# Triangular inverse of the chunked recurrence: blocks of 32 instead of 64 on TensorE, and an order that counts changes of tile size

## The reference, cut to what matters

```python
def step(S, inp):
    r_t, w_t, k_t, v_t, kk_t, b_t = inp
    sa = jnp.einsum('bhvk,bhk->bhv', S, kk_t)
    S = (S * w_t[:, :, None, :] - sa[..., None] * b_t[:, :, None, :]
         + v_t[..., None] * k_t[:, :, None, :])
    return S, jnp.einsum('bhvk,bhk->bhv', S, r_t)
```

## Time and profile before

| | |
|---|---|
| time, median of 3 runs | 3736.47 us (3733.08 to 3736.66) |
| the profiled execution | 3741.04 us, span 3739.3 us |
| mean granted TensorE clock | 0.97 |
| PE busy in the span | 3506.3 us (94%) |
| DVE busy | 1892.1 us (51%) |
| ACT busy | 945.0 us (25%) |
| DMA | 177.54 MB, mean 47 GB/s |

### The profile page before, as it was taken

The page is one execution under the profiler, slowest core; times in us unless marked ns, Lnnn a source line. Parts: engine busy times, 40 slices in busy tenths (PEclk is TensorE's granted clock), DMA queues, the critical chain, the costliest instruction groups (busy, mean ns, idle before and its releaser), DMA issues.

```text
span 3739.3 us, 63595 instructions
## 1 busy us (share of the span) xinstructions
PE 3506.3 (94%) x28813; PEld 2205.1 (59%) x28813; DVE 1892.1 (51%) x2750; ACT 945.0 (25%) x1867; POOL 49.4 (1%) x114
## 2 busy tenths in 40 slices
PE   7998879989999999789999999998899698999988
PEld 2445655549989899444444444445566345777753
DVE  2037746435555554645555540115999653444524
ACT  3006640125455555220000000100111302233310
POOL 2000000000000000100000000000000000000000
PEclk9999999989999999899999999999999899999999
DMA  6001003200000000321111121113111012010021
GB/s 229 0 14 54 1 23 135 81 6 18 4 18 4 4 4 4 110 94 64 67 57 45 43 93 40 57 51 96 34 34 56 11 63 58 23 34 23 1 84 62
DMA packets 110626, 177.54 MB, mean 47 GB/s; under 512 B 5379, under 2 KB 66562, under 8 KB 109714
## 3 DMA queue, kind: packets, MB, share of 16 engines
q1 hardware_dynamic: 101218, 141.59, 11.3%
q10 hardware_dynamic: 9136, 31.87, 2.4%
HBM read 147.23 MB, written 26.21 MB: 46 GB/s over the span
## 4 chain that ended last, share of the span: by engine, by line
PE 85%; DVE 9%; ACT 4%; DMA 2%; issue 1%; ACTq 0%; SPq 0%; DVEq 0%
PE psum_all L66 83%; ACT sbuf_all L75 3%; DVE sbuf_all L94 3%; DVE sbuf_all L84 2%; DVE sbuf_all L102 2%; PE psum_all L69 1%; ACT L75 1%; DMA sbuf_all<-in_w_mod 1%; DVE sbuf_all L91 0%; DMA sbuf_all<-in_gla_w_out 0%; DVE sbuf_all L108 0%; DMA sbuf_all<-in_w_up 0%; DVE sbuf_all L97 0%; DMA yd_spill<-sbuf_all 0%; DMA sbuf_all<-in_conv_w_in 0%
## 5 line engine op out<-in xcount | busy, mean ns | idle before, releaser
L66 PE MATMUL psum_all<-sbuf_all 64*64 64x64 f32 (+12 forms) x28042 | 3406.6, 306 | 183.4 <-ACT sbuf_all L75 57.6
L66 PEld LDWEIGHTS psum_all<-sbuf_all 64*64 64x64 f32 (+5 forms) x28042 | 2120.3, 153 | 1446.2 <-issue 1032.3
L75 ACT ACTIVATE sbuf_all<-psum_all 128x512 f32<-128x512 f32 (+5 forms) x925 | 409.4, 462 | 1543.4 <-PE psum_all L66 1428.9
L94 DVE SCALAR_TENSOR_TENSOR sbuf_all<-sbuf_all 128x1040 f32<-128x1040 f32 (+8 forms) x571 | 623.5, 1094 | 25.1 <-PE psum_all L66 4.9
L84 DVE TENSOR_TENSOR sbuf_all<-sbuf_all 128x512 f32<-128x512 f32 (+10 forms) x593 | 470.3, 817 | 165.1 <-ACT sbuf_all L75 121.3
L75 ACT ACTIVATE sbuf_all<-sbuf_all 128x64 f32<-128x64 f32 (+10 forms) x454 | 260.9, 584 | 856.4 <-DVE sbuf_all L78 355.2
L78 DVE COPY sbuf_all<-psum_all 128x256 f32<-128x256 f32 (+5 forms) x137 | 71.0, 526 | 472.7 <-PE psum_all L66 459.3
L75 ACT ACTIVATE sbuf_all<-psum_all,sbuf_all 128x1280 f32<-128x1280 f32 (+5 forms) x212 | 163.9, 781 | 342.4 <-PE psum_all L66 326.1
L84 DVE TENSOR_TENSOR sbuf_all<-sbuf_all,psum_all 128x512 f32<-128x512 f32 (+3 forms) x160 | 102.0, 640 | 274.4 <-PE psum_all L66 273.3
L108 DVE COPY_PREDICATED sbuf_all<-sbuf_all,psum_all 128x256 f32<-128x256 int32 (+2 forms) x296 | 145.6, 493 | 159.5 <-PE psum_all L66 154.8
L69 PE MATMUL psum_all<-sbuf_all 128*128 128x128 f32 (+2 forms) x771 | 109.5, 281 | 38.5 <-DVE sbuf_all L84 9.5
(11 more groups left out here) (19 smaller groups left out, 140.6 us busy)
## 6 DMA issues: line engine op xcount, KB each, us to landing
sbuf_all<-in_w_mod SPq DMA_DIRECT2D x12, 2048.0 KB, 8.3
sbuf_all<-in_w_up SPq DMA_DIRECT2D x22, 1024.0 KB, 7.7
sbuf_all<-in_w_in SPq DMA_DIRECT2D x6, 2048.0 KB, 8.9
x_spill<-sbuf_all SPq DMA_DIRECT2D x16, 512.0 KB, 2.9
sbuf_all<-in_conv_w_in SPq DMA_DIRECT2D x16, 512.0 KB, 6.3
sbuf_all<-in_gla_w_in SPq DMA_DIRECT2D x8, 1024.0 KB, 5.3
sbuf_all<-in_w_down SPq DMA_DIRECT2D x4, 1792.0 KB, 7.4
hid_spill<-sbuf_all ACTq DMA_DIRECT2D x9, 512.0 KB, 2.6
```

What stands on the lines that cost most here:

```text
L66: return self.e.matmul(out, lhsT, rhs, start=start, stop=stop, skip_group_check=True)
L75: return self.e.activation(out, in_, func, bias=bias, scale=scale, **kw)
L94: return self.e.scalar_tensor_tensor(out, a, s, b, op0, op1) if self.e is not None else Unissued()
```

## The change

Levels 1 to 4 combine blocks that lie within blocks of 32. Before, they were computed on the whole 64x64 matrices, of which all but the diagonal blocks of 32 are zero. Now D and E of these levels are kept compact: 128 partitions by 4 chunks by 32 columns, four blocks of 32 on the partitions (two heads, two diagonal blocks each), and each matmul is 32x32 weights by 32 columns on one quarter of the partitions (`QUARTERS`). So `first_turn` and `level_y` have 16 small matmuls where there were 8, `level_de` 32 where there were 16.

The last level, from blocks of 32 to blocks of 64, becomes two products of 8 small matmuls, `last_y` and `last_e`, from one quarter of the partitions to its neighbour. `spread` (VectorE, two predicated copies) puts the compact E back on the diagonal of the full one, `last_turn` (VectorE) copies the first product, and `last_out` (VectorE) puts the new corner into the full E. `de_out` of the last level on ScalarE falls away. The copies out of PSUM are half as wide as before at levels 1 to 4. The masks are rebuilt for blocks of 32 on GpSimd in the stage before, in more and smaller operations (16 instead of the 4 that copied `half_level`).

The costs in the scheduler's table are new (for instance 280 ns for `level_y` in place of 500), TensorE is charged `CHANGE` = 90 ns when a step has another tile size than the one before it, and `PACE` is 3600 instead of 5000. So the order of the steps is another one on all three engines.

```diff
-SCAN_LEVELS = range(1, 6)
+SCAN_LEVELS = range(1, 5)
+QUARTERS = [(slice(32 * n, 32 * n + 32), 32 * (n % 2)) for n in range(4)]
...
-PACE = 5000
+PACE = 3600
...
+BY_32 = ("first_turn", "level_y", "level_de", "last_y", "last_e")
+OTHER_TILES = ("key_norms", "key_spread", "gates")
+CHANGE = 90
...
-        step("t", 500, ("first_turn", gi), ("first", gi))
-        step("s", 390, ("first_out", gi), ("first_turn", gi))
+        step("t", 280, ("first_turn", gi), ("first", gi))
+        step("s", 300, ("first_out", gi), ("first_turn", gi))
         for li in SCAN_LEVELS:
...
+            step("t", 280, ("level_y", gi, li), ("first_out", gi) if li == 1 else ("de_out", gi, li - 1))
+            step("v", 330, ("turn", gi, li), ("level_y", gi, li))
+            step("t", 530, ("level_de", gi, li), ("turn", gi, li))
+            step("s", 390, ("de_out", gi, li), ("level_de", gi, li))
+        done = ("de_out", gi, SCAN_LEVELS[-1])
+        step("v", 400, ("spread", gi), done)
+        step("t", 280, ("last_y", gi), done)
+        step("v", 300, ("last_turn", gi), ("last_y", gi))
+        step("t", 280, ("last_e", gi), ("last_turn", gi))
+        step("v", 330, ("last_out", gi), ("last_e", gi), ("spread", gi))
+        step("t", 500, ("solve", gi), ("last_out", gi), ("turned_out", gi, 0), ("turned_out", gi, 1))
...
+                    change = e == "t" and tile_mode(name[0]) != mode
+                    choices.append((max(at, free[e] + CHANGE * change), due[name], name[1:], name))
...
             for u in range(4):
-                for rows in HALVES:
-                    done = te.matmul(bank[rows, u * C:(u + 1) * C], g["A"][rows, u, 0:64], g["D"][rows, u, :])
+                for rows, b in QUARTERS:
+                    done = te.matmul(bank[rows, u * 32:u * 32 + 32], g["A"][rows, u, b:b + 32], g["D"][rows, u, :])
             done.then_inc(*T.tick("level_y", gi, li))
...
+            old = lambda rows, b, u: g["E"][rows, u, b:b + 32] if li == 1 else g["E32"][rows, u, :]
             for u in range(4):
-                for rows in HALVES:
-                    done = te.matmul(bank[rows, 256 + u * C:256 + (u + 1) * C], turn[rows, u, :], g["E"][rows, u, :])
+                for rows, b in QUARTERS:
+                    te.matmul(bank[rows, u * 32:u * 32 + 32], old(rows, b, u), turn[rows, u, :])
+            for u in range(4):
+                for rows, b in QUARTERS:
+                    done = te.matmul(bank[rows, 128 + u * 32:160 + u * 32], turn[rows, u, :], old(rows, b, u))
             done.then_inc(*T.tick("level_de", gi, li))
+        elif kind == "last_y":
...
+            for u in range(4):
+                for (rows, _), (to, b) in zip(*sides(STREAMS[GROUPS[gi][0]][1])):
+                    done = te.matmul(bank[to, u * 32:u * 32 + 32], g["A"][rows, u, b:b + 32], g["D"][rows, u, :])
+            done.then_inc(*T.tick("last_y", gi))
...
+        elif kind == "spread":
...
+            for b in range(2):
+                ve.predicated(g["E"][:, :, 32 * b:32 * b + 32], K.side_mask[:, b, :].bitcast(I32).unsqueeze(1).broadcast_to([P, 4, 32]),
+                              g["E32"]).then_inc(*V.tick("spread", gi))
```

More of the change, by code:

```diff
@@ L1077, in project_pool @@
             ge.wait_ge(*G.now())
-            ge.copy(K.half_level[d][rows], side[rows, 0:6, h * 64:(h + 1) * 64]).then_inc(*G.tick())
+            ge.copy(K.first_level[d][rows], side[rows, 0, h * 64:(h + 1) * 64]).then_inc(*G.tick())
+    ge.wait_ge(*G.now())
+    ge.memset(K.side_mask, 0.0).then_inc(*G.tick())
+    for n in range(4):
+        rows, cols = slice(32 * n, 32 * n + 32), slice(32 * n, 32 * n + 32)
+        for d in range(2):
+            ge.wait_ge(*G.now())
+            ge.copy(K.turn_mask[d][rows], K.level["lower" if d == 0 else "upper"][rows, 1:5, cols]).then_inc(*G.tick())
+        ge.wait_ge(*G.now())
+        ge.copy(K.quarter_ident[rows, :], K.ident[rows, cols]).then_inc(*G.tick())
+        ge.wait_ge(*G.now())
+        ge.memset(K.side_mask[rows, n % 2, :], 1.0).then_inc(*G.tick())
     ge.wait_ge(*G.now())
@@ L1141, in group_chunks, with tile_mode @@
     return chunk_order(s)[4 * n:4 * n + 4]
-PACE = 5000
+PACE = 3600
 HALF = ((0, 640), (640, 1280))
 EVACUATED = {"key_norms": "key_roots", "key_spread": "key_scale", "gates": "gate_out", "bonus": "bonus_out", "products": "mask", "first_turn": "first_out",
-             "turned": "turned_out", "level_y": "turn", "level_de": "de_out", "solve": "solve_out"}
+             "turned": "turned_out", "level_y": "turn", "level_de": "de_out", "last_y": "last_turn", "last_e": "last_out",
+             "solve": "solve_out"}
+BY_32 = ("first_turn", "level_y", "level_de", "last_y", "last_e")
+OTHER_TILES = ("key_norms", "key_spread", "gates")
+CHANGE = 90
+TURN_READ = {"turn": "level_de", "last_turn": "last_e"}
+def tile_mode(kind):
+    return 32 if kind in BY_32 else 128 if kind in OTHER_TILES else 64
 def scan_steps():
@@ L1545, in scan_vector @@
     chunked = lambda x: x.rearrange("p (n t) -> p n t", t=C)
-    turns, last_turn = K.turn_level, {}
+    turn_user = {}
     c3, lw3, t13, aa3, kk3 = (chunked(x) for x in (cc, lw, t1, aa, K.kk))
@@ L1829, in scan_pool @@
         for turn in side:
-            ge.copy(turn, K.half_ident.unsqueeze(1).broadcast_to([P, 4, C])).then_inc(*K.scan.g.tick("turn_levels"))
+            ge.copy(turn, K.quarter_ident.unsqueeze(1).broadcast_to([P, 4, 32])).then_inc(*K.scan.g.tick("turn_levels"))
 def scan_sync(K, sy):
```

115 lines of the change are left out of this document (73 added, 42 removed).

## The result

The changed kernel takes 3939.89 us (median of 4 runs, 3937.37 to 3943.67) against 3736.56 us for the kernel before on the same chip: ratio 1.0545, 95% interval 1.0527 to 1.0564. It is 5.4% slower, 203 us, where 76 us less was forecast. The profiled execution has a span of 3935.6 us. The end of the recurrence moved from 1509.9 to 1709.3 us, 199 us later, so the whole loss lies in the changed stretch; the forecast had it at 1434.

A forecast was written before the change was run, and what follows sets the result against it. The prediction took TensorE, busy 94% of the span, as the bound: 3741 us, less 101 (127 saved, 26 for changes), plus 25 of waits, gives 3665; 4.6 us lower for the median, 3661, range 3625 to 3712.

The forecast's parts named there:

- the round of four: 32x32 level work on TensorE: four records, one on each quarter, in 32 ns; 153 us with two-quarter rounds, against 280 before.
- a term that the prediction put at nothing: TensorE's granted clock in the recurrence: a fall below 0.98 was named as possible and priced at nothing.
- 26 us of changes: TensorE's order in the recurrence: 288 more changes of tile size at 0.09 us each, bounds 0 and 43 us.
- 25 of waits: New TensorE waits for other engines in the recurrence: 25 us added, bounds 0 and 50.
- The signs named for being wrong: 32x32 windows under 100 or 65 records a us, VectorE or ScalarE over 25% of the chain, or clock clearly below 0.98.
- Rival 2: 32x32 work on TensorE: issuing eight instructions makes a round about 44 ns, not 32; 3704 us, chance 0.10.
- The bound above: Upper limit for a round of four on TensorE: 58 ns, if smaller size gives nothing but four still overlap.
- Rival 3: 32x32 work on TensorE: quarters don't overlap as halves do, a round takes 64 ns; 3774 us, chance 0.05.
- Rival 4: TensorE's small matmuls: every record keeps its 29 ns whatever its size; about 4005 us, chance 0.01.
- Rival 1: VectorE and ScalarE take back TensorE's gain through new waits of 55 to 85 us; middle 3706 us, chance 0.15.
- The last sign of error: TensorE's granted clock clearly below the 0.98 of before, since TensorE would be less busy; priced at nothing.

The follow-up runs named there:

- e11_busy64: The changed kernel with every product on blocks of 32 moving 64 columns in place of 32, same matmul count and order, values wrong; 3938.63 us, ratio 1.054.
- e9_busy: The changed kernel with all its matmuls kept, every product on blocks of 32 moving 128 columns in place of 32, values wrong; 3997.69 us, ratio 1.0695.
- e12_busy64c0: The changed kernel with 64 columns in each product on blocks of 32 and CHANGE = 0, values wrong; 3889.87 us, ratio 1.0402.
- e2_wide: The changed kernel with half the matmuls on blocks of 32, each moving 64 columns, values of half the chunks wrong; 3705.0 us, ratio 0.9908.
- e1_lab: The kernel before with stretches of matmuls that wait for nothing ahead of the recurrence, for its trace only; 640 records of 32x32 took 15.8 us.
- e3_change0: The changed kernel with CHANGE = 0, so 595 changes of tile size instead of 375; 3894.37 us, ratio 1.042.
- e5_wide4: The changed kernel with a quarter of the matmuls on blocks of 32, each moving 128 columns, values of three chunks of four wrong; 3654.09 us, ratio 0.9778.
- e6_realcost: The changed kernel with the scheduler's TensorE costs set to what the instruction supply gives and PACE 5000; 3948.68 us, ratio 1.0567.
- e8_lab2: The kernel before with longer stretches of matmuls that wait for nothing, for its trace; 2560 records on four quarters took 70.5 us.

## Why the prediction was wrong

**The step that failed** is the round of four under "TensorE, term by term": 4160 rounds on four quarters at 32 ns and 640 on two at 32 ns, 153 us. The array does start a round of four in 33 ns. But the level work has 8960 matmuls, 17920 records, 35840 instructions with the loads: 140 blocks, at 3.45 us each 483 us. Put in the place of the 153, that makes 697.9 - 280 + 483 = 901 us for the recurrence, and 897.3 were measured.

That it comes so near is luck. By this sum the 32x32 work takes 483 us and the rest 418; in the trace they take 379 and 517 (table under e11_busy64). So the term of 153 us was 226 too small, not 330: small matmuls also live on blocks that came in while the others ran. The other 100 us are the rest at the lower clock, a term that the prediction put at nothing; in e9_busy, with the clock up, the same work takes 416. That the two trade against each other at nearly the same total e11_busy64 and e12_busy64c0 show, and so the count of instructions is what the loss goes back to. The sum for e2_wide, 70 blocks, is near in the same way (697.9 - 280 + 242 = 660, 663.5 measured), and it leaves out the 26 us of changes and 25 of waits that the prediction added. The row was in the profile all along: 226 packets of the instruction queue, and for 1000 to 1100 us of the kernel before

```profile
q8 instruction: 21, 0.34, 1.5%
```

a packet every 4.8 us; unbroken 64x64 work takes one every 3.74 (256 x 14.6 ns). There was next to nothing to gain by more and shorter matmuls. The signs named for being wrong show it too: at 128 records in 3.45 us there are 37 records of 32x32 a us, far under the 65 of rivals 3 and 4, though for neither's reason, and the idle time before them is 126 us, 115 of it issue, where tens were to be right. I read transfers as data only, and wrote that none is near the path.

**Why the rest doesn't make up for it.** If the supply had run on evenly beside all work, the 213 packets of the recurrence would have needed 213 x 3.45 = 735 us, and not 897. But at full clock the 64x64 work takes an instruction every 14.6 ns, hardly slower than the supply gives them, and only about two blocks are ahead, so there is little reserve for the small matmuls. This is worked out from e1_lab; e3_change0 and e12_busy64c0 agree, where more mixing gave back 45 and 49 us.

**Rival 2** named the issue of eight instructions, but priced it at 44 ns a round, from halfway to the bound of 58 ns. The bound was taken from pairs, four instructions; the same rate for eight is 117 ns, and the measured mean of a long stretch is 110 (70.5 us for 640 rounds). So it named nearly the right thing, at 12 of the 78 ns a round that it cost. The bound above was wrong by treating the round, not the instruction, as the unit. **Rival 3** fell: four quarters do overlap. **Rival 4** gave 4005 us by 29 ns a record, near in size, and for small records in a long row nearly right as a mean (27.5); but its reason, a floor between starts, is not what happens: within a burst records start every 8 ns. The rule of the Trainium skill that I cited there, from "TensorE: Matmul & The Clock Gate", is contradicted across tiles as it was in the earlier trace rows. The Trainium skill does describe the blocks, in "Runtime: NRT & Kernel Launch", section "Instruction fetch mechanics": 256 instructions in 16 KiB, fetched in sequence while others are executed. It calls the cost mostly hidden; here it is 1.2 to 2.6 us a block for such tiles.

**Rival 1**, VectorE and ScalarE, fell: their waits together didn't grow (26 us against 28), and e5_wide4 reached 3654 with the same copies.

**Terms that held.** Changes: in TensorE's records the first start after a change from 64x64 to 32x32 comes 0.098 us later than normal at full clock, the way back 0.095, against my 0.09. Predicated copies of 128x128: 303 ns (305). The copies of `spread`: 315 ns, where I took 250. ScalarE's 128x256: 386 (384). The hand-over at the end is 1.49 us a chunk, as the earlier trace rows:

```profile
1698.35 0.30 DVE sbuf_all L94
1698.64 0.04 issue
1698.69 1.13 PE psum_all L66 x24
1699.82 0.02 issue
1699.84 0.30 DVE sbuf_all L94
```

The last sign of error that I had named, a granted clock below 0.98, came true (0.76 in the long window). I had priced it at nothing. It costs the work outside 32x32 some 100 us, but e11_busy64 and e12_busy64c0 show that the total hardly gets shorter when it is up.

**Open.** Why a block takes 3.45 us and at times 3.73 or 4.00; that the beat is the fetch itself is inferred from bursts and packets having one size and one spacing, since no run could change the fetch. Whether the total would stay the same with 32 columns and the clock up. Why e5_wide4's recurrence took 612 us: that is 63 above 697.9 - 280 + 1200 x 0.109 = 549, and 12 above the 600 that the prediction's changes and waits make of it; part may be the lower clock (100 us at the lower level against 51). And e6_realcost.

## What to carry to other kernels

Before a matmul is split into smaller tiles, count TensorE's instructions, four for each float32 matmul, and not only its columns: here 256 of them take 3.45 us to arrive in the steady bursts, so a long stretch of work below about 13.5 ns an instruction runs no faster, whatever the array could do. Smaller tiles pay if the moving side is made wider at the same time, so that the number of matmuls falls. e2_wide and e5_wide4 show that gain, but they leave out products: here each chunk has weights of its own, and the algorithm would have to allow the sharing. A scheduler that groups small matmuls made it worse (e3_change0). When an estimate halves the time of a dense stretch, compare the packets of the instruction queue in that stretch with its new length.

## What the runs showed of the hardware

- A granted clock of 0.60 in 15.3 us of unbroken matmuls on one quarter of the array (1.00 for the first 2.8 us, then 0.50), and 1.00 in 18.7 us on one half alone. What sets it I can't tell from two stretches.
- TensorE's instructions come as packets of 256 on a queue of their own, one in 3.45 us in steady bursts, and some two are ahead (e1_lab, e8_lab2).
- A change of tile size costs 0.09 to 0.14 us at full clock, and as much if only the number of columns changes (64x32 against 64x64).
- A wait on a semaphore that is already fulfilled takes TensorE 47 ns.
